# Expert gathers in a two-layer PEER model: down and up rows side by side, one 8 KB gather per pick in eight slots, two picks at a time

## The chip, the cores and the metric

One core of a Trainium2 chip runs the whole program. The metric is device time in microseconds (us). Each run of the kernel before gives one time; three runs were made.

## The reference

The model has two layers and a third part with sparse attention, linear attention and a mixture of experts. The change touches only the feed-forward of the two layers, which looks up single rows of large tables:

```
def peer_ffn(h, w_q, sub_keys, down, up):
    def one_block(xb):                          # 128 tokens; there are two such blocks
        q = (xb @ w_q).reshape(n, 8, 2, 128)    # 8 heads, 2 halves of a key
        s = einsum('thpk,pnk->thpn', q, sub_keys)
        s_top, i_top = top_k(s, 16)
        ... the best 16 of the 16 x 16 sums -> idx, gate = softmax(best_s)
        u = take(down, idx, axis=0)             # 16 picks for each of 8 heads, rows of 1024 floats
        act = gelu(einsum('thkd,td->thk', u, xb))
        v = take(up, idx, axis=0)
        return einsum('thk,thkd->td', gate * act, v)
```

Each token picks 8 heads x 16 = 128 experts out of 16384. For each of them it needs a row of `down` (4 KB in float32), whose dot product with the token gives a weight, and the row of `up` with the same index (4 KB), which is added to the output with that weight. A layer has 256 tokens, so 128 picks x 2 blocks of 128 tokens = 256 gathers of `down` and 256 of `up`, each of 128 rows (512 KB): 268 MB in a layer.

## The kernel before

The program is written engine by engine, with semaphores between them. In each layer `peer(l)` does this part. Tokens lie on the 128 partitions; `t` is the block of 128 tokens, a group `g` (0 to 15) is one head of one block, and `k` (0 to 15) is a pick within it. So a gather brings, for one (g, k), one row to each partition.

**GpSimd (POOL)** issues all gathers as indirect DMAs in the order of `gather_order()`: first the 16 down rows of group 0, then down rows of group g and up rows of group g-1 in turn, and the 16 up rows of the last group at the end. There are 16 slots of 4 KB a partition (`gslot`): eight in `G_arena`, eight in two buffers of the weight ring that are lent to the gathers for the length of the stage. Before the gather number i is issued, POOL waits until the gather i-16 has been used: by DVE if it was a down row, by TensorE if it was an up row. Slots 8 to 11 are open from query 1 on, slots 12 to 15 from query 3 on, since the ring buffers hold the query weights until then.

**DVE** does the dots (`down(g)`, one `scalar_tensor_tensor` of 128x1024 with an accumulated sum, line 1253). Between the dots it works off the search for the next heads' indices, `top_k`, in 15 steps, one after each of the first three picks of every four. At the end of a group it does `weight(g)`: the 16 activations times the gates. At the end of the layer `mix_last` adds eight of the last 16 up rows on DVE.

**ScalarE (ACT)** applies gelu to the 16 dots of a group at once, and then makes the diagonals (line 823): for each pick a 128x128 matrix with that pick's weights on its diagonal, in four buffers.

**TensorE (PE)** multiplies the diagonal by the up row, two matmuls of 512 columns for each pick (line 1971), and sums all 128 picks of a block in two PSUM banks. A float32 matmul shows as two records. Ahead of this, PE runs the eight queries (`query(s)`, line 1714, 64 records each) and their scores (line 1927), all before the first up row.

**Layer 0 has more in it**: in the shadow of the gathers PE works out the modulation of layer 1 (`mod_parts`, line 1771, and `mod_total`), one of 10 chunks at the end of each group from group 4 on. ACT copies their results out (lines 702 and 709), and SP loads the weights of a later chunk (2 MB, line 548) when the semaphore `modp` says that a chunk is used. Layer 1 has two such chunks.

At the end `add_experts` multiplies the two banks of a block by a gain and adds them to `x`.

Of the kernel before, what the change touches and what calls it, by code (L numbers as in the profile page):

```python
# [22 lines left out]
NT = T // P  # L23
# [8 lines left out]
GSLOTS = 16  # L32
# [43 lines left out]
def query_no(l, s):  # L76

    return 9 * l + s + 2
# [28 lines left out]

def hidden(l, g):

    c = HIDDEN[l].start + g - SHADOW  # L110
    return [c] if c in HIDDEN[l] else []


def gather_order():

    order = [("down", 0, k) for k in range(GSLOTS)]
    for g in range(1, BLOCKS):
        for k in range(GSLOTS):
            order += [("down", g, k), ("up", g - 1, k)]
    return order + [("up", BLOCKS - 1, k) for k in range(GSLOTS)]  # L120


ORDER = gather_order()
PLACE = {pick: i for i, pick in enumerate(ORDER)}


LAST_MIXED = (1, 3, 5, 7, 9, 11, 12, 13)
LAST_UP = tuple(k for k in range(GSLOTS) if k not in LAST_MIXED)
UPS = GSLOTS * (BLOCKS - 1) + len(LAST_UP)


def up_picks(g):

    return range(GSLOTS) if g < BLOCKS - 1 else LAST_UP


def up_no(l, g, k):

    return UPS * l + GSLOTS * g + up_picks(g).index(k) + 1

# [65 lines left out]
def program(nc, a, out):  # L206

    ctx = ExitStack()
    with ctx:
# [93 lines left out]
        G_arena = pe_(8, D)  # L303
# [7 lines left out]
        mixed_up = qb.rearrange("p a b c -> p (a b c)")[:, D:2 * D]  # L311
# [49 lines left out]
        def lend(l):  # L361

            lent[l] = turn[0:2]
            for _ in range(2):
                enter(None, ("x_peer", NT * (l + 1)))
            for k in lent[l]:
                turn.remove(k)
# [47 lines left out]
        def gslot(l, kind, g, k):  # L415

            n = PLACE[kind, g, k] % GSLOTS
            if n < 8:
                return G_arena[:, n]
            return ring[:, lent[l][(n - 8) // 4], 1024 * (n % 4):1024 * (n % 4) + 1024]  # L420

        def wait_gathered(eng, l, kind, g, k):
            i = PLACE[kind, g, k]
            eng.wait_ge(S[f"gathered{i % GSLOTS}"], 16 * ((len(ORDER) * l + i) // GSLOTS + 1))

# [99 lines left out]
        def _(sp):  # L525
# [62 lines left out]
            sp.wait_ge(S["up_used"], UPS)  # L588
# [10 lines left out]
            sp.wait_ge(S["up_used"], 2 * UPS)  # L599
# [30 lines left out]
        @block.gpsimd  # L630
        def _(pool):
            for l in range(2):
                for i, (kind, g, k) in enumerate(ORDER):
                    t, hh = g // 8, g % 8
                    if kind == "down" and k == 0:
                        pool.wait_ge(S["idx_ready"], 9 * l + (g // 2 + 2 if g else 1))
                    if i >= GSLOTS:
                        before, of, j = ORDER[i - GSLOTS]
                        if before == "down":
                            pool.wait_ge(S["down_used"], GSLOTS * (BLOCKS * l + of) + j + 1)  # L640
                        else:
                            pool.wait_ge(S["up_used"], up_no(l, of, j))
                    elif i >= 8 and i % 4 == 0:
                        pool.wait_ge(S["pq"], query_no(l, 2 * ((i - 8) // 4) + 1))
                    elif l and i == 0:
                        pool.wait_ge(S["x_peer"], NT * l)
                    pool.indirect_dma_start(  # L647
                        out=gslot(l, kind, g, k), out_offset=None, in_=a[kind],
                        in_offset=bass.IndirectOffsetOnAxis(ap=idx_all[:, t, 16 * hh + k:16 * hh + k + 1], axis=0)).then_inc(
                        S[f"gathered{i % GSLOTS}"], 16)  # L650
# [3 lines left out]
        def _(act_):  # L654
# [110 lines left out]
            def peer(l):  # L765
# [39 lines left out]
                for s in range(2, 8):  # L805
                    query_out(s)
                    score_out(s - 1)
                score_out(7)

                def gelu(g):  # L810
                    t, hh = g // 8, g % 8
                    part = act[:, t, 16 * hh:16 * hh + 16]
                    act_.wait_ge(S["down_used"], GSLOTS * (BLOCKS * l + g + 1))
                    act_.activation(part, part, ACT.Gelu_apprx_tanh).then_inc(S["peer_gelu"], 1)

                def diagonals(g):
                    t, hh = g // 8, g % 8
                    act_.wait_ge(S["peer_w"], BLOCKS * l + g + 1)
                    for k in up_picks(g):
                        n = up_no(l, g, k)  # L820
                        if n > 4:
                            act_.wait_ge(S["up_used"], n - 4)
# [3 lines left out]
                for g in range(BLOCKS + 1):  # L826
                    if g < BLOCKS and g % 2 == 0:
                        t, c = g // 8, (g // 2) % 4
                        part = gate[:, t, 32 * c:32 * c + 32]
                        act_.wait_ge(S["gate_in"], 8 * l + g // 2 + 1)  # L830
                        act_.activation(part, part, ACT.Exp).then_inc(S["gate_exp"], 1)
                    if g:
                        diagonals(g - 1)
                    if g < BLOCKS:
                        gelu(g)
                    if l == 0 and g == 11:
                        act_.wait_ge(S["x_peer"], 1)
                        tile_sum(x, h, 0)
                    if l == 0 and g == 13:
                        tile_root("n1_1", 0)  # L840
                    if g == BLOCKS:
                        root_table()
                    for c in hidden(l, g - 1):
                        mod_part_out(1, c, 0)
                    for c in hidden(l, g - 2):
                        mod_total_out(1, c, 0)
# [132 lines left out]
        def _(v):  # L979
# [205 lines left out]
            def peer(l):  # L1185
# [54 lines left out]
                def gates(m):  # L1240
# [5 lines left out]
                    link(v.tensor_tensor(g3, g3, bc(gsum[:, 1], 2, 16), ALU.mult))  # L1246

                def down(g):
                    t, hh = g // 8, g % 8
                    for k in range(GSLOTS):  # L1250
                        row = gslot(l, "down", g, k)
                        wait_gathered(v, l, "down", g, k)
                        v.scalar_tensor_tensor(out=row, in0=row, scalar=1.0, in1=h[:, t], op0=ALU.mult,  # L1253
                                               op1=ALU.mult, accum_out=act[:, t, 16 * hh + k:16 * hh + k + 1]).then_inc(
                            S["down_used"], 1)
                        n = GSLOTS * (g % 2) + k
                        if g < BLOCKS - 2 and n % 4 < 3 and n - n // 4 < STEPS:
                            top_k(g // 2 + 1, n - n // 4)

                def weight(g):  # L1260
                    t, hh = g // 8, g % 8
                    v.wait_ge(S["peer_gelu"], BLOCKS * l + g + 1)
                    part = act[:, t, 16 * hh:16 * hh + 16]
                    v.tensor_tensor(part, part, gate[:, t, 16 * hh:16 * hh + 16], ALU.mult).then_inc(S["peer_w"], 1)

                def add_experts(t):
                    v.wait_ge(S["up_used"], up_no(l, 7, GSLOTS - 1) if t == 0 else UPS * (l + 1))
# [4 lines left out]

                def mix_last():
                    t, g = NT - 1, BLOCKS - 1
                    v.wait_ge(S["peer_w"], BLOCKS * (l + 1))
                    for i, k in enumerate(LAST_MIXED):
                        w = act[:, t, 16 * (g % 8) + k:16 * (g % 8) + k + 1]
                        wait_gathered(v, l, "up", g, k)
                        if i:
                            link(v.scalar_tensor_tensor(out=mixed_up, in0=gslot(l, "up", g, k), scalar=w, in1=mixed_up,  # L1280
                                                        op0=ALU.mult, op1=ALU.add))
                        else:
                            link(v.tensor_scalar(mixed_up, gslot(l, "up", g, k), w, None, ALU.mult))
                    link(v.tensor_tensor(mixed_up, mixed_up, mod[:, 5], ALU.mult))
                    link(v.tensor_tensor(x[:, t], x[:, t], mixed_up, ALU.add))
# [5 lines left out]
                for g in range(BLOCKS):  # L1291
                    down(g)
                    if g % 2 == 0:
                        gates(g // 2)
                    weight(g)
# [7 lines left out]
                    if l == 0 and g == 14:  # L1303
# [5 lines left out]
                        tile_norm("n1_1", 0, x, h, mod[:, 1], mod[:, 0])  # L1309
                if l == 0:  # L1310
# [6 lines left out]
                v.wait_ge(S["pq_ev"], query_no(l, 7))  # L1317
# [1030 lines left out]
```

## Time and profile before

| | |
|---|---|
| three runs | 2755.77, 2758.12 and 2764.55 us, median 2758.12 us |
| profiled execution | span 2868.3 us from its first to its last instruction |
| instructions | 22121 |
| gather stage of layer 0 | first gather issued at 282.0 us, last up row's matmuls end at about 1083 us |
| gather stage of layer 1 | first gather at 1131.7 us, last up row's matmuls end at 1919.9 us |
| busy shares of the span | PE 79%, DVE 41%, ACT 17%, POOL 39% |
| queue of the gathers | 536.94 MB, 49.3% of what 16 DMA engines could do in the span |

The profiled execution is 110 us longer than the median of the three runs. All rows are from it. The line numbers are those of the kernel before. A DMA share of 1.0 means that all 16 DMA engines had packets all the time; GB/s is what they moved. "PEclk" is the granted TensorE clock as a share of full speed: 1.00 is 2.4 GHz and 0.50 is 1.2 GHz. "Idle before" is the time in which an engine did nothing ahead of an instruction, and the arrow names what ended it; "issue" means nothing that the profile shows, "remote" another core or a queue that it does not know.

### The profile page before, as it was taken

Reading aid. Unit: us, or ns where it says so; the run is one execution under the profiler, and the core shown is the slowest. Engines: PE = TensorE matmul, PEld = TensorE weight load, DVE = VectorE, ACT = ScalarE, POOL = GpSimd, SP = SyncE. Lnnn points to the kernel's source line nnn. Section 1 sums busy time; section 2 is a strip of 40 time slices with the busy share of each in tenths; the row PEclk is TensorE's granted clock in tenths of the full one; section 3 lists DMA queues with packets and bytes.
Section 4 is the critical chain, followed back from the end, with each engine's and each line's share of the span. In section 5 each row is a group of like instructions: output and inputs, shape, how many; then the busy total and the mean of one; then the engine's idle time right before and its main releaser. Section 6 shows DMA issues by size and latency. Waiting matters only on the chain.

```text
span 2868.3 us, 22121 instructions
## 1 busy us (share of the span) xinstructions
PE 2268.7 (79%) x7843; PEld 1064.3 (37%) x7843; DVE 1180.9 (41%) x2875; ACT 494.1 (17%) x1074; POOL 1117.8 (39%) x1028
## 2 busy tenths in 40 slices
PE   6998876676776877977567776759997989998997
PEld 2455722222232336722123222224454544344443
DVE  1243665555556445665556555440043421010101
ACT  2141111121111211211111111120124111000001
POOL 0000577776776761577767777750000000000000
PEclk9998899988898888999979998989998889999999
DMA  8433899999999985899979999994410059999996
GB/s 321 164 140 119 287 365 368 353 401 385 383 401 396 378 335 199 288 355 360 382 288 356 364 374 351 377 340 155 171 66 0 1 221 393 393 395 393 393 393 245
DMA packets 292278, 864.12 MB, mean 301 GB/s; under 512 B 19372, under 2 KB 26668, under 8 KB 291912
## 3 DMA queue, kind: packets, MB, share of 16 engines
q0 software_dynamic: 147456, 536.94, 49.3%
q1 hardware_dynamic: 144712, 325.74, 30.5%
q8 instruction: 66, 1.08, 0.2%
q14 instruction: 44, 0.36, 0.0%
HBM read 861.55 MB, written 1.05 MB: 301 GB/s over the span
## 4 chain that ended last, share of the span: by engine, by line
PE 43%; DMA 16%; POOL 16%; issue 11%; another core or an unknown queue 5%; DVE 4%; ACT 3%; SPq 2%; POOLq 0%; DVEq 0%; ACTq 0%
PE bank L1714 17%; PE bank L1971 12%; DMA arena<-in_w_up 9%; POOL ring L647 8%; POOL arena L647 8%; DMA ring<-in_up,arena 5%; PE bank L2223 5%; PE bank L1723 2%; SPq L619 2%; DMA arena<-in_up,arena 2%; PE bank L1771 1%; PE bank L2266 1%; PE bank L1783 1%; PE bank L1784 1%
## 5 line engine op out<-in xcount | busy, mean ns | idle before, releaser
L1971 PE MATMUL bank<-arena 128*128 128x512 f32 x992 | 508.2, 654 | 228.8 <-ACT arena L823 112.5
L1971 PE MATMUL bank<-ring,arena 128*128 128x512 f32 x992 | 496.7, 635 | 170.7 <-DMA ring<-in_up,arena 100.4
L1253 DVE SCALAR_TENSOR_TENSOR ring<-ring,h 128x1024 f32<-128x1024 f32 x256 | 313.0, 1225 | 307.8 <-DMA ring<-in_down,arena 233.4
L647 POOL DMA_INDIRECT arena<-in_down,arena x256 | 261.6, 1022 | 439.4 <-DVE arena L1237 348.7
L1253 DVE SCALAR_TENSOR_TENSOR arena<-arena,h 128x1024 f32<-128x1024 f32 x256 | 313.5, 1226 | 263.4 <-DMA arena<-in_down,arena 179.5
L1971 PEld LDWEIGHTS bank<-arena 128*128 128x128 f32 x992 | 193.8, 207 | 540.5 <-issue 380.7
L1971 PEld LDWEIGHTS bank<-ring,arena 128*128 128x128 f32 x992 | 182.1, 197 | 478.1 <-issue 269.0
L647 POOL DMA_INDIRECT arena<-in_up,arena x256 | 288.2, 1126 | 146.5 <-PE bank L1971 61.5
L823 ACT ACTIVATE arena<-const,arena 128x128 f32<-128x128 f32 x496 | 188.3, 398 | 855.0 <-PE bank L1971 500.2
L647 POOL DMA_INDIRECT ring<-in_up,arena x256 | 292.7, 1143 | 103.8 <-issue 68.6
L647 POOL DMA_INDIRECT ring<-in_down,arena x256 | 275.1, 1074 | 104.3 <-issue 77.4
L1714 PE MATMUL bank<-ring,hT 128*128 128x512 f32 (+2 forms) x640 | 256.0, 563 | 3.0 <-ACT hT L693 2.2
L2223 PE MATMUL bank<-ring,arena 128*64 128x512 f32 x768 | 233.3, 604 | 29.2 <-DMA arena<-in_w_up 28.0
L1714 PEld LDWEIGHTS bank<-ring,hT 128*128 128x128 f32 x640 | 124.4, 195 | 133.1 <-issue 125.3
L1678 DVE TENSOR_TENSOR arena<-arena,bank 128x512 f32<-128x512 f32 x16 | 11.0, 689 | 341.1 <-PE bank L2223 341.1
L1714 PE MATMUL bank<-hT,ring 128*128 128x128 f32 x1024 | 130.5, 289 | 15.9 <-issue 12.8
L2223 PEld LDWEIGHTS bank<-ring,arena 128*64 128x64 f32 x768 | 73.0, 139 | 178.7 <-issue 177.3
L1714 PEld LDWEIGHTS bank<-hT,ring 128*128 128x128 f32 x1024 | 127.2, 205 | 18.7 <-issue 16.5
L2223 PE MATMUL bank<-arena 128*64 128x512 f32 x256 | 121.3, 630 | 0.0
L2266 PE MATMUL bank<-ring,arena 128*64 128x512 f32 x256 | 113.3, 595 | 9.1 <-DVE arena L1680 9.1
L2266 PE MATMUL bank<-arena 128*64 128x512 f32 x256 | 113.3, 595 | 0.0
L1723 PE MATMUL bank<-const 128*128 128x512 f32 x186 | 88.1, 630 | 0.0
(400 smaller groups left out, 1873.5 us busy)
## 6 DMA issues: line engine op xcount, KB each, us to landing
ring<-in_w_gate SPq DMA_DIRECT2D x32, 2048.0 KB, 22.3
ring<-in_mod_w SPq DMA_DIRECT2D x24, 2048.0 KB, 15.2
ring<-in_w_up SPq DMA_DIRECT2D x16, 2048.0 KB
arena<-in_w_up SPq DMA_DIRECT2D x16, 2048.0 KB, 19.9
ring<-in_w_down SPq DMA_DIRECT2D x16, 2048.0 KB, 14.3
arena<-in_w_down SPq DMA_DIRECT2D x16, 2048.0 KB, 19.0
ring<-in_w_in SPq DMA_DIRECT2D x9, 2048.0 KB, 7.6
ring<-in_peer_w_q SPq DMA_DIRECT2D x8, 2048.0 KB, 11.5
```

The source lines that it names most:

```text
L619: sp.dma_start(w_moe[3 * k + j].rearrange("p (k n) -> p k n", k=kk), a[w][2 * i + k].rearrange("(k p) n -> p k n", p=P)).then_inc(moe_land ...
L647: pool.indirect_dma_start(out=gslot(l, kind, g, k), out_offset=None, in_=a[kind], in_offset=bass.IndirectOffsetOnAxis(ap=idx_all[:, t, 16 ...
L823: act_.activation(diag[:, n % 4], ident, ACT.Copy, scale=act[:, t, 16 * hh + k:16 * hh + k + 1]).then_inc(S["diag_made"], 1)
L1253: v.scalar_tensor_tensor(out=row, in0=row, scalar=1.0, in1=h[:, t], op0=ALU.mult, op1=ALU.mult, accum_out=act[:, t, 16 * hh + k:16 * hh + ...
L1714: ins = pe.matmul(dst, lhsT, rhs, start=i == 0, stop=i == len(pairs) - 1)
L1723: pe.matmul(bank[b][:, :], ones, cst("causal"), start=True, stop=True)
L1771: ins = pe.matmul(bank[4 * l + n % 2][32 * j:32 * j + 32, :], (cB2 if ctx else cB)[:, 2 * j + k], w[:, 2 * j + k], start=k == 0, stop=k == ...
L1783: pe.matmul(bank[4 * l + 2 + n % 2][:, :], ones, mpart[:, n % 2], start=True, stop=False)
L1784: pe.matmul(bank[4 * l + 2 + n % 2][:, :], ones[row:row + 1], bias, start=False, stop=True).then_inc(S["mod"], 1)
L1971: ins = pe.matmul(bank[2 * t + c][:, :], diag[:, n % 4], row[:, 512 * c:512 * c + 512], start=hh == 0 and k == 0, stop=hh == 7 and k == up ...
L2223: ins = pe.matmul(bank[2 + j][CAP * k:CAP * k + CAP, :], xs[:, q, CAP * k:CAP * k + CAP], w_k[3 * k + j][:, q], start=q == 0, stop=q == KT ...
L2266: ins = pe.matmul(bank[c][CAP * k:CAP * k + CAP, :], hsel[:, f, CAP * k:CAP * k + CAP], w_k[3 * k + 2][:, f, 512 * c:512 * c + 512], start ...
```

## The change

- The host lays `down` and `up` side by side in one table, `experts`, of 8 KB rows. One gather per pick brings both rows (1 MB in all). A layer issues 256 gathers and not 512.
- There are eight slots of 8 KB in the place of 16 of 4 KB. The bytes are the same.
- The work goes in groups `j` of two picks (`PER = 2`), 128 to a layer. POOL waits before every second gather, and for TensorE alone: the pair of slots is free when the up matmuls of the pair four places earlier are done (`slot_free`).
- ACT applies gelu to two dots at a time (`weigh`) and makes no diagonals.
- DVE makes the diagonals, with activation and gate multiplied in the same `tensor_scalar`, right behind the dots of the next pair: `diagonals(j-1)` follows the second dot of pair `j`. It waits for the gelu of its pair and, since there are two pairs of diagonal buffers, for the matmuls of two pairs earlier.
- PE does the matmuls of a pair on one wait. Queries 4 to 7 move from ahead of the stage to behind pairs 3, 7, 11 and 15, and their scores one pair later.
- `mix_last` goes: all up rows are summed on PE.
- SP's loads that waited for query 7 and for the last up row wait for the same events, at their new places.

```diff
-GSLOTS = 16
+GSLOTS = 8
+HEAD = 16
...
+LATE_QUERIES = {3: 4, 7: 5, 11: 6, 15: 7}
...
+PER = 2
+GROUPS = PICKS * NT // PER
+
+def slot_free(l, n):
+    return GROUPS * l + (n - GSLOTS) // PER + 1
...
-        G_arena = pe_(8, D)
+        G_arena = pe_(4, 2 * D)
...
                 # GpSimd
+                for n in range(PICKS * NT):
...
+                    if n >= GSLOTS:
+                        if n % PER == 0:
+                            pool.wait_ge(S["up_used"], slot_free(l, n))
+                    elif n >= 4 and n % 2 == 0:
+                        pool.wait_ge(S["pq"], query_no(l, n - 3))
...
                     pool.indirect_dma_start(
-                        out=gslot(l, kind, g, k), out_offset=None, in_=a[kind],
+                        out=gslot(l, n), out_offset=None, in_=a["experts"],
...
                 # ScalarE
+                def weigh(j):
+                    t, at = PER * j // PICKS, PER * j % PICKS
+                    part = act[:, t, at:at + PER]
+                    act_.wait_ge(S["down_used"], GROUPS * l + j + 1)
+                    act_.activation(part, part, ACT.Gelu_apprx_tanh).then_inc(S["peer_gelu"], 1)
...
-                        act_.activation(diag[:, n % 4], ident, ACT.Copy, scale=act[:, t, 16 * hh + k:16 * hh + k + 1]).then_inc(
-                            S["diag_made"], 1)
...
                 # DVE
+                def diagonals(j):
+                    t, at = PER * j // PICKS, PER * j % PICKS
+                    v.wait_ge(S["peer_gelu"], GROUPS * l + j + 1)
+                    if j % HEAD == 0:
+                        v.wait_ge(S["gates"], 8 * l + j // HEAD + 1)
+                    if j >= 2:
+                        v.wait_ge(S["up_used"], GROUPS * l + j - 1)
+                    for k in range(PER):
+                        ins = v.tensor_scalar(diag[:, PER * (j % 2) + k], ident, act[:, t, at + k:at + k + 1],
+                                              gate[:, t, at + k:at + k + 1], ALU.mult, ALU.mult)
+                    ins.then_inc(S["diag_made"], 1)
...
                 def down(g):
+                    for k in range(HEAD):
+                        row = gslot(l, HEAD * g + k)[:, 0:D]
+                        wait_gathered(v, l, HEAD * g + k)
...
+                        if k % PER == PER - 1:
+                            ins.then_inc(S["down_used"], 1)
+                            if g or k >= PER:
+                                diagonals((HEAD * g + k) // PER - 1)
...
-                def weight(g):
-                def mix_last():
...
                 # TensorE
+                for j in range(GROUPS):
...
+                    pe.wait_ge(S["diag_made"], GROUPS * l + j + 1)
+                    for k in range(PER):
+                        row = gslot(l, PER * j + k)[:, D:2 * D]
...
+                    ins.then_inc(S["up_used"], 1)
+                    if j in LATE_QUERIES:
+                        query(LATE_QUERIES[j])
+                    if j - 1 in LATE_QUERIES:
+                        scores(LATE_QUERIES[j - 1])
```

## Rows read from the trace of the kernel before

**Rows 1.** The page: span, POOL and PE busy, the gathers' queue.
```profile
span 2868.3 us, 22121 instructions
PE 2268.7 (79%) x7843; PEld 1064.3 (37%) x7843; DVE 1180.9 (41%) x2875; ACT 494.1 (17%) x1074; POOL 1117.8 (39%) x1028
...
q0 software_dynamic: 147456, 536.94, 49.3%
```

**Rows 2.** Busy time by stretch: engine busy us (count), last PEclk, DMA share, GB/s.
```profile
282.00:350.00 68.00, 57.25 (x464) 55.50 (x463) 41.11 (x132) 12.55 (x22) 38.85 (x33) 0.91 0.76 266
350.00:600.00 250.00, 179.91 (x371) 64.97 (x369) 148.35 (x358) 42.05 (x102) 190.08 (x170) 0.96 0.98 367
600.00:1050.00 450.00, 336.97 (x790) 127.85 (x788) 246.22 (x552) 82.48 (x193) 316.56 (x302) 0.89 1.00 390
1200.00:1900.00 700.00, 498.34 (x1005) 183.49 (x1004) 391.37 (x905) 116.23 (x281) 516.27 (x471) 0.92 0.95 357
```

**Rows 3.** Timeline of layer 1, a steady stretch: start, length, engine, instruction, idle before.
```profile
1401.46 1.48 POOL L647 DMA_INDIRECT ring<-in_down,arena  x1 [0.30 <-issue]
...
1402.19 1.98 PE L1971 MATMUL bank<-arena 128*128 128x512 f32 x4 [0.57 <-DMA arena<-in_up,arena]
...
1407.04 0.99 POOL L647 DMA_INDIRECT ring<-in_down,arena  x1 [0.30 <-issue]
...
1408.34 0.94 POOL L647 DMA_INDIRECT ring<-in_up,arena  x1 [0.31 <-issue]
1408.56 1.23 DVE L1253 SCALAR_TENSOR_TENSOR ring<-ring,h 128x1024 f32<-128x1024 f32 x1 [1.33 <-DMA ring<-in_down,arena]
...
1409.58 1.02 POOL L647 DMA_INDIRECT ring<-in_down,arena  x1 [0.30 <-issue]
```

**Rows 4.** Groups of instructions between 1200 and 1900 us: busy, mean ns, idle before.
```profile
L1229 DVE TENSOR_TENSOR cols<-const,cols 128x512 f32<-128x512 f32 x14 | 9.6, 689 | 0.0
...
L1041 DVE MATCH_REPLACE8 gvec<-cols,gvec 128x128 f32<-128x128 f32 x16 | 4.3, 276 | 1.3 <-issue 1.3
...
L1217 DVE TENSOR_SCALAR cols<-cols 128x32 uint32<-128x32 uint32 x6 | 1.0, 174 | 0.0
```

**Rows 5.** Timeline of layer 1 around a restart of the gathers.
```profile
1490.53 0.60 ACT L702 ACTIVATE hT<-bank 128x512 f32<-128x512 f32 x1 [19.88 <-remote]
...
1492.05 10.09 PE L1971 MATMUL bank<-arena 128*128 128x512 f32 x16 [15.72 <-ACT arena L823]
...
1495.84 0.40 ACT L823 ACTIVATE arena<-const,arena 128x128 f32<-128x128 f32 x1 [3.07 <-PE bank L1971]
1496.08 0.94 POOL L647 DMA_INDIRECT arena<-in_up,arena  x1 [7.20 <-PE bank L1971]
1497.32 0.94 POOL L647 DMA_INDIRECT arena<-in_down,arena  x1 [0.30 <-issue]
...
1502.57 1.23 DVE L1253 SCALAR_TENSOR_TENSOR arena<-arena,h 128x1024 f32<-128x1024 f32 x1 [7.11 <-DMA arena<-in_down,arena]
```

**Rows 6.** Two stretches of 2 us in the mixture of experts: 2 KB rows, then 4 KB rows.
```profile
2396.00:2398.00 2.00, 1.43 (x10) 0.63 (x10) 1.80 (x6) 0.85 (x2) 0.00 (x0) 1.00 1.03 383
2414.00:2416.00 2.00, 2.00 (x10) 0.77 (x11) 0.00 (x0) 0.00 (x0) 0.00 (x0) 1.00 1.03 412
```

**Rows 7.** Timeline of PE in layer 0: queries 4 and 5 and their neighbours' scores.
```profile
310.68 7.31 PE L1714 MATMUL bank<-hT,ring 128*128 128x128 f32 x64
317.82 1.06 PE L1927 MATMUL bank<-cols,arena 128*128 128x128 f32 x8
318.72 7.31 PE L1714 MATMUL bank<-hT,ring 128*128 128x128 f32 x64
325.86 1.06 PE L1927 MATMUL bank<-cols,arena 128*128 128x128 f32 x8
```

**Rows 8.** Stretches of 10 us: eight of layer 1's 70 are under 300 GB/s.
```profile
1260.00:1270.00 10.00, 9.93 (x17) 4.28 (x18) 9.86 (x23) 2.06 (x6) 8.18 (x7) 0.70 0.76 252
...
1490.00:1500.00 10.00, 7.95 (x12) 3.46 (x13) 2.47 (x4) 3.04 (x8) 2.81 (x3) 0.60 0.50 177
...
1880.00:1890.00 10.00, 8.82 (x15) 3.37 (x14) 3.91 (x9) 2.41 (x6) 6.42 (x7) 0.64 0.86 297
```

**Rows 9.** Waits of ACT, layer 0, then layer 1: us in total, times, longest.
```profile
ACT hT L702 <- remote: 92.3, 8, 18.7
...
ACT hT L702 <- remote: 40.4, 2, 20.5
```

**Rows 10.** Timeline of the end of layer 1's gathers.
```profile
1911.03 0.94 POOL L647 DMA_INDIRECT ring<-in_up,arena  x1 [0.30 <-issue]
...
1916.21 3.70 PE L1971 MATMUL bank<-ring,arena 128*128 128x512 f32 x8 [3.13 <-DMA ring<-in_up,arena]
...
1921.45 1.22 DVE L1271 TENSOR_TENSOR x<-x,arena 128x1024 f32<-128x1024 f32 x1
```

More of the change, by code:

```diff
@@ L111, in hidden @@
     return [c] if c in HIDDEN[l] else []
[L114 to L139, printed above, removed]
+PER = 2
+GROUPS = PICKS * NT // PER
+def slot_free(l, n):
+    return GROUPS * l + (n - GSLOTS) // PER + 1
 def operand(tag, n):
@@ L587, in _ @@
             load_gain(4)
-            sp.wait_ge(S["up_used"], UPS)
+            sp.wait_ge(S["up_used"], GROUPS)
             load_weights("pool", 1)
@@ L826, in peer @@
[L826 to L836, printed above, removed]
+                query_out(2)
@@ new lines, in peer, with gate_out @@
+                score_out(1)
+                query_out(3)
+                score_out(2)
+                score_out(3)
+                def weigh(j):
+                    t, at = PER * j // PICKS, PER * j % PICKS
+                    part = act[:, t, at:at + PER]
+                    act_.wait_ge(S["down_used"], GROUPS * l + j + 1)
+                    act_.activation(part, part, ACT.Gelu_apprx_tanh).then_inc(S["peer_gelu"], 1)
+                def gate_out(m):
+                    t, c = m // 4, m % 4
+                    part = gate[:, t, 32 * c:32 * c + 32]
+                    act_.wait_ge(S["gate_in"], 8 * l + m + 1)
+                    act_.activation(part, part, ACT.Exp).then_inc(S["gate_exp"], 1)
@@ new lines, in peer @@
+                gate_out(0)
+                for j in range(GROUPS):
+                    g, i = j // 8, j % 8
+                    weigh(j)
+                    if j in LATE_QUERIES:
+                        query_out(LATE_QUERIES[j])
+                    if j - 1 in LATE_QUERIES:
+                        score_out(LATE_QUERIES[j - 1])
+                    if j % HEAD == 8 and j // HEAD < 7:
+                        gate_out(j // HEAD + 1)
+                    for c in hidden(l, g - 1):
+                        if i == 1:
+                            mod_part_out(1, c, 0)
+                        if i == 5:
+                            mod_total_out(1, c, 0)
+                    if l == 0 and (g, i) == (11, 0):
@@ L837, in peer @@
                         act_.wait_ge(S["x_peer"], 1)
                         tile_sum(x, h, 0)
-                    if l == 0 and g == 13:
+                    if l == 0 and (g, i) == (13, 0):
                         tile_root("n1_1", 0)
[L841 to L846, printed above, removed]
+                root_table()
@@ L1248, in down @@
                 def down(g):
                     t, hh = g // 8, g % 8
[L1250 to L1258, printed above, removed]
@@ L1260, in weight @@
-                def weight(g):
[L1261 to L1264, printed above, removed]
+                    for k in range(HEAD):
+                        row = gslot(l, HEAD * g + k)[:, 0:D]
+                        wait_gathered(v, l, HEAD * g + k)
+                        ins = v.scalar_tensor_tensor(out=row, in0=row, scalar=1.0, in1=h[:, t], op0=ALU.mult,
+                                                     op1=ALU.mult, accum_out=act[:, t, HEAD * hh + k:HEAD * hh + k + 1])
+                        if k % PER == PER - 1:
+                            ins.then_inc(S["down_used"], 1)
+                            if g or k >= PER:
+                                diagonals((HEAD * g + k) // PER - 1)
+                        n = HEAD * (g % 2) + k
+                        if g < BLOCKS - 2:
+                            if n % 4 < 3 and n - n // 4 < STEPS:
+                                top_k(g // 2 + 1, n - n // 4)
+                            if n == 24:
+                                gates(g // 2 + 1)
+                        if g == 0 and k == 1:
+                            gates(0)
@@ L1309, in peer @@
                         tile_norm("n1_1", 0, x, h, mod[:, 1], mod[:, 0])
+                diagonals(GROUPS - 1)
                 if l == 0:
```

129 lines of the change are left out of this document (45 added, 84 removed).

## The prediction

> **What bounds the kernel now.** I read the page first. PE is the busiest engine by the share of the span, and the gathers' queue holds 49.3% of the DMA engines' time [rows 1]. Busy time by stretch puts that share where it belongs: in both gather stages the DMA engines stand at 0.95 to 1.00 while PE is at about 0.7, so these stages, 55% of the span, are paced by the gathers [rows 2]. The timeline of a steady stretch shows two limits that fall together. POOL issues a gather every 1.24 to 1.31 us and waits for nobody between (idle 0.30 us each time): two gathers in 2.54 us. That is 1.05 MB in 2.54 us, 413 GB/s, and 410 GB/s is also about what the DMA engines reach elsewhere with 4 KB rows [rows 3, 6]. A down row issued at 1401.46 us is used at 1408.56 us, 7.1 us later. Its slot is needed again only 16 gathers (20 us) after its issue. So before, a slot has some 12 us to spare.
>
> Layer 1 between 1200 and 1900 us moves 357 GB/s, not 410 [rows 2]: 13% or 90 us are lost. Eight stretches of 10 us under 300 GB/s hold 35 us of it [rows 8]; they are restarts after a wait like that of ACT on line 702 [rows 5]. The other 55 us are POOL's: 471 issues took 516 us, 1.10 us each against 0.94 undisturbed [rows 2, 3], and with 0.30 between them that is 1.40 us a gather where the DMA engines need 1.28.
>
> **What goes.** 256 of 512 POOL issues in a layer. POOL then needs 1.4 us for a pick of which the transfer takes 2.56, so it paces nothing any more. At most this returns the 55 us in layer 1, and less in layer 0, where the 2 MB weight loads from another queue fill the DMA engines (390 GB/s). ACT's diagonals, `weight` and `mix_last` go too. They lie beside the transfers and are worth nothing in the sum.
>
> **What it costs: the loop.** A slot is now held from its issue until PE has used the pair, and diagonals of pair j wait for the dots of j+1. So the gathers of pair j+4 are issued after the matmuls of j, and those need pair j+1 landed: one turn of the loop moves the work on by three pairs. Its terms, with an otherwise quiet queue:
> - PE's end to POOL's issue: 0.25 us (1495.84, when ACT is let go, to 1496.08) [rows 5].
> - Issue to use of a gather of 0.5 MB: 5.25 us (1497.32 to 1502.57), and 5.2 us for the last one (1911.03 to 1916.21) [rows 5, 10]. For 1 MB I add 1.28 us, and 2.56 us for the second of the pair behind the first: 9.05 us. The bound above is the 7.1 us of the full queue in place of 5.2 [rows 3], 11 us; the bound below is 8 us, if a microsecond of the 5.2 was the gather ahead.
> - The second dot: 1.23 us [rows 3].
> - Two diagonals on DVE. No row shows a `tensor_scalar` of 128x128 in float32. It lies between 0.17 us (128x32) and 0.28 us (another operation of 128x128) [rows 4]. I take 0.22, 0.45 us a pair; the ends are 0.35 and 0.55.
> - The way to PE 0.1 us, and two picks of 1.98 us that overlap by 0.26: 3.7 us [rows 3].
>
> Sum: 14.8 us for three pairs, 4.9 a pair. On top comes what DVE has in hand when the second row lands. A step of `top_k` is 0.9 to 2.1 us (three operations of 0.69 us in the longest) [rows 4] and goes behind 15 of 32 picks. The row may have to wait for it, or POOL's first issue may take 1.5 us. I put 0.8 us on a turn: 15.6 us, 5.2 us a pair. The DMA engines need 2.10 MB / 410 GB/s = 5.1 us for a pair. Two limits so close do not simply give the larger one; any late step on either side is kept. I take 5.25 us (bounds 5.0 and 5.9).
>
> The diagonal is also the place where the Trainium skill speaks against the change: "SBUF — State Buffer", in its list of which operations grab the shared port pair, says that a float32 `tensor_scalar` within SBUF can keep GpSimd from writing descriptors. POOL's issues do range up to 1.48 us beside DVE's work [rows 3]. By the rule an issue that met both diagonals would take 0.45 us more, and by the loop's order none meets its own pair's, since POOL is waiting for PE then; the sum would be the same by both.
>
> **What it costs: the start.** Before, 18 MB have moved 68 us after the first gather (266 GB/s) [rows 2]. After, the last two of eight slots open when query 3 ends, at 310.7 us [rows 7], and are full at 317; no slot comes free before PE's first pair. DVE can weigh that pair once the scores and the exponentials of the gates are out, some 5 us behind query 3. Four pairs at about 4.1 us of DVE (two dots, two diagonals, one or two steps) and 5.5 us from dot to matmuls put pair 3's end at 337, 55 us after the first gather. Then four queries stand in the loop, each 7.15 us, and four scores of 0.9 to 1.06 [rows 7]. From pair 3 the matmuls of pair 4 wait for query 4 (R + 10.9 us), then 9.3 us for the gather of pair 8 and 5.5 for the dots, diagonals and matmuls of pair 7: 25.7 us for four pairs, and not 21. Four such rounds end with pair 19 at 55 + 103 = 158 us. The remaining 108 pairs at 5.25 us are 567 us: 725 us a layer. In layer 0 ten weight loads of 2 MB add 5.1 each, 52 us. The end is even: last landing to `x` takes 1.23 + 0.45 + 3.8 + 2.7 = 8.2 us, before 6.5 [rows 10].
>
> **The sum.** In the profile, layer 1's stage is 788 us before. After it is 725 us, plus the gaps. These hold 35 us today and stay, since what makes them (the waits on line 702 and their like) is not touched, and each restart now begins with a whole pair at half clock, as PE's first 16 records take 10.1 us where four at full clock take 1.98 [rows 5, 3], with no slot in hand: 3 us more each. So 725 + 35 + 24 = 784, no change. Layer 0 comes to 725 + 52 + 25 = 802 against 801. But the profiled execution is 110 us above the median run. It is likeliest that this excess lies in the waits without a visible cause: line 702 alone waits 92 us in layer 0 and 40 in layer 1 [rows 9]. Then before, a timed run spends about 1589 - 110 = 1479 us in both stages, and after, with no gaps, 2 x 725 + 52 = 1502: 23 us slower. If the excess lies elsewhere, the change is worth nothing. I take 22 us: 2758 + 22 = 2780 us.
>
> **The rivals.**
> - *The loop is longer.* If a gather of a pair lands like one of the full queue (11 us and not 9.05), a turn is 17.5 us, 5.85 a pair: 216 x 0.6 = 130 us more, 2890. Half of that is 2840. For it: the loop has no slack, and a weight load in layer 0 doubles the time of a transfer. Against: the queue is shallower, with at most 4 MB waiting of 8. It decides from a turn of 16.5 us up.
> - *Faster: the loop stays under the transfers.* If the landing takes 8 us and DVE's steps hide in the 2.5 us between two rows, a turn is 14.3 us and the DMA engines pace. Going from 2 KB to 4 KB rows took them from 383 to 412 GB/s [rows 6], which is 10 us of fixed time per 1000 packets; with 8 KB it would be 424, 4.95 us a pair. 216 x 0.3 = 65 us less than my sum, 2715. It decides below a turn of 15 us. "DMA: Bandwidth & Descriptors" of the Trainium skill (Anatomy of one DMA) would have it so: 2.0 us fixed plus bytes at 436 GB/s, by which an estimate for the second of the pair is 6.8 us. The rows have 5.2 us for half a megabyte, where that rule gives 3.2.
> - *Faster: the gaps shrink.* Line 702's waits grow while POOL goes on filling 16 slots (8 MB, 20 us of transfers). Now POOL stops after a pair or two. If the waits are also in the timed runs, and half of their 132 us goes with half of the depth, that is up to 50 us: 2710 to 2745. Against: the chain behind them has no slack, so what is shorter in the wait is paid in the restart.
> - *No change*: gains on POOL and losses at the start cancel, as in the profile's sum: 2750 to 2766.
>
> **Numbers.** Slower as forecast (2767 to 2830) 0.35, longer loop 0.17, no change 0.13, transfers pace 0.20, gaps shrink 0.15. What a measurement can tell from no change is 0.3%, 8 us. Faster 0.35, same 0.13, slower 0.52. The range leaves out 0.1 on either side: 2695 to 2870. The likeliest case alone is 2767 to 2830.
>
> **What would show it.** Right: POOL's gathers in steady stretches wait for PE (line 1971 renamed), not 0.30 "issue"; DMA share between 0.93 and 0.99 there; first issue of a pair to its second dot about 9 us; pairs every 5.2 us; in the first 16 pairs PE is nearly always busy and POOL idle for 7 us around each query. Wrong: a DMA share of 1.0 at over 415 GB/s with POOL's waits short of the transfers (faster), or landings of 11 us with shares under 0.9 (much slower). What would break the forecast most is the landing term, since each microsecond in it is a third of a microsecond a pair, 72 us in all, and the part of the 110 us excess that timed runs have too.

## The result

The changed kernel takes 2874.22 us (median of four runs, 2868.83 to 2882.88); the kernel before took 2761.34 us beside it (2755.77 to 2765.86). The ratio is 1.042, 95% interval [1.039, 1.045]: 113 us slower, where 22 were forecast, and 4 us above the end of the range. A later set of seven runs gave 2873.83 us again, but the kernel before stood at 2853.16 us in that set, ratio 1.007 [1.005, 1.009]. So the kernel before has two levels, near 2758 and near 2853 us, one to each set of runs (a set ran on one chip); the changed kernel showed one in these two sets.

First the page of the changed kernel, answering to [rows 1].

```profile
span 2867.0 us, 21606 instructions
PE 2301.3 (80%) x7907; PEld 1094.2 (38%) x7907; DVE 1283.7 (45%) x3335; ACT 350.3 (12%) x802; POOL 565.1 (20%) x516
...
q0 software_dynamic: 73728, 536.90, 47.5%
```

POOL's work is halved and half the packets carry the same bytes, yet the span of this execution is that of the profiled one before (2868.3 us). Busy time by stretch, answering to [rows 2]; the columns are engine busy us (count), PEclk, DMA share, GB/s.

```profile
282.00:440.00 158.00, 126.52 (x621) 83.51 (x620) 89.13 (x263) 16.80 (x40) 44.55 (x44) 0.92 0.77 293
440.00:600.00 160.00, 117.28 (x239) 45.62 (x238) 105.07 (x263) 12.17 (x35) 58.92 (x54) 0.90 0.96 381
600.00:1050.00 450.00, 340.97 (x793) 131.27 (x792) 290.39 (x727) 38.81 (x110) 179.72 (x151) 0.92 0.98 386
1134.00:1300.00 166.00, 132.42 (x648) 88.17 (x646) 94.43 (x280) 16.80 (x40) 45.05 (x46) 0.93 0.74 288
1300.00:1900.00 600.00, 436.93 (x880) 171.20 (x881) 398.23 (x998) 40.62 (x128) 226.86 (x209) 0.91 0.95 373
```

Long after the start, layer 1 moves 373 GB/s, a pair (2.10 MB) in 5.62 us. The forecast had 5.25. No engine is full. The waits of that last stretch say who waits for whom (us in total, times, longest; those of ACT and of PE's weight loads are left out):

```profile
POOL ring L631 <- PE bank L1948: 180.1, 52, 8.6
PE bank L1948 <- DVE arena L1237: 164.7, 81, 4.7
POOL arena L631 <- PE bank L1948: 155.1, 52, 8.0
DVE ring L1246 <- DMA ring<-in_experts,arena: 117.5, 97, 4.1
DVE arena L1246 <- DMA arena<-in_experts,arena: 82.8, 79, 3.9
```

That is a closed ring: POOL waits for PE, PE for DVE's diagonals, DVE for the transfers, and these for POOL. The timeline of layer 1, a stretch without steps of `top_k` (start, length, engine, instruction, idle before), answers to [rows 3]:

```profile
1846.26 1.86 POOL L631 DMA_INDIRECT ring<-in_experts,arena  x1 [2.50 <-PE bank L1948]
1847.23 0.60 DVE L1237 TENSOR_SCALAR arena<-const,arena 128x128 f32<-128x128 f32 x2
...
1847.88 3.70 PE L1948 MATMUL bank<-ring,arena 128*128 128x512 f32 x8 [1.90 <-DVE arena L1237]
1848.42 0.94 POOL L631 DMA_INDIRECT ring<-in_experts,arena  x1 [0.30 <-issue]
...
1851.86 1.56 POOL L631 DMA_INDIRECT ring<-in_experts,arena  x1 [2.49 <-PE bank L1948]
...
1855.14 1.23 DVE L1246 SCALAR_TENSOR_TENSOR ring<-ring,h 128x1024 f32<-128x1024 f32 x1 [2.01 <-DMA ring<-in_experts,arena]
...
1857.63 1.23 DVE L1246 SCALAR_TENSOR_TENSOR ring<-ring,h 128x1024 f32<-128x1024 f32 x1 [1.26 <-DMA ring<-in_experts,arena]
...
1858.78 0.60 DVE L1237 TENSOR_SCALAR arena<-const,arena 128x128 f32<-128x128 f32 x2
...
1859.44 3.70 PE L1948 MATMUL bank<-arena 128*128 128x512 f32 x8 [2.55 <-DVE arena L1237]
```

Follow one turn. The pair issued at 1846.26 has its dots at 1855.14 and 1857.63, 8.9 and 11.4 us later, both ended by the transfers. Then come the diagonals of the pair ahead of it, 3.70 us of PE, and at 1863.41 the next issue into slots of this turn: 17.15 us, three pairs further on, 5.7 us each.

### The profile page after: what moved, and what is told of

Read it like the earlier page. It is cut to its first block, busy times and chain, and to the rows that moved or that the text cites. A ratio compares the mean times of both kernels' runs of the same rounds, so it can differ in the third digit from the quotient of the medians.

```text
span 2867.0 us, 21606 instructions
## 1 busy us (share of the span) xinstructions
PE 2301.3 (80%) x7907; PEld 1094.2 (38%) x7907; DVE 1283.7 (45%) x3335; ACT 350.3 (12%) x802; POOL 565.1 (20%) x516
## 4 chain that ended last, share of the span: by engine, by line
PE 46%; DMA 33%; DVE 7%; issue 6%; POOL 3%; ACT 3%; SPq 2%; DVEq 0%; POOLq 0%; ACTq 0%
PE bank L1948 16%; PE bank L1691 16%; DMA arena<-in_experts,arena 13%; DMA ring<-in_experts,arena 10%; DMA arena<-in_w_up 10%; PE bank L2206 5%; PE bank L1700 2%; SPq L602 2%; DVE arena L1237 2%; POOL ring L631 1%; PE bank L1748 1%; POOL arena L631 1%; DVE arena L1246 1%; PE bank L1760 1%; PE bank L1761 1%
## 5 line engine op out<-in xcount | busy, mean ns | idle before, releaser
L1948 PE MATMUL bank<-ring,arena 128*128 128x512 f32 x1024 | 535.5, 674 | 219.2 <-DVE arena L1237 219.2
L631 POOL DMA_INDIRECT arena<-in_experts,arena x256 | 275.9, 1078 | 858.5 <-PE bank L1948 469.3
L1948 PEld LDWEIGHTS bank<-ring,arena 128*128 128x128 f32 x1024 | 210.6, 214 | 540.9 <-DVE arena L1237 308.2
L631 POOL DMA_INDIRECT ring<-in_experts,arena x256 | 289.0, 1129 | 478.9 <-PE bank L1948 416.8
L1948 PEld LDWEIGHTS bank<-arena 128*128 128x128 f32 x1024 | 200.2, 205 | 473.4 <-DVE arena L1237 258.9
L799 ACT ACTIVATE arena<-arena 128x2 f32<-128x2 f32 x256 | 51.1, 203 | 1205.6 <-DVE ring L1246 621.3
L1237 DVE TENSOR_SCALAR arena<-const,arena 128x128 f32<-128x128 f32 x512 | 153.6, 343 | 79.8 <-ACT arena L799 79.3
L1691 PE MATMUL bank<-hT,ring 128*128 128x128 f32 x1024 | 123.9, 284 | 3.0 <-ACT hT L759 3.0
L1748 PE MATMUL bank<-ring,hT 128*32 128x512 f32 x448 | 60.6, 669 | 13.6 <-DMA ring<-in_mod_w 12.8
## 6 DMA issues: line engine op xcount, KB each, us to landing
ring<-in_mod_w SPq DMA_DIRECT2D x24, 2048.0 KB, 17.2
```

The source lines that it names most:

```text
L631: pool.indirect_dma_start(out=gslot(l, n), out_offset=None, in_=a["experts"], in_offset=bass.IndirectOffsetOnAxis(ap=idx_all[:, t, at:at + ...
L1237: ins = v.tensor_scalar(diag[:, PER * (j % 2) + k], ident, act[:, t, at + k:at + k + 1], gate[:, t, at + k:at + k + 1], ALU.mult, ALU.mult)
L1691: ins = pe.matmul(dst, lhsT, rhs, start=i == 0, stop=i == len(pairs) - 1)
L1748: ins = pe.matmul(bank[4 * l + n % 2][32 * j:32 * j + 32, :], (cB2 if ctx else cB)[:, 2 * j + k], w[:, 2 * j + k], start=k == 0, stop=k == ...
L1948: ins = pe.matmul(bank[2 * t + c][:, :], diag[:, PER * (j % 2) + k], row[:, 512 * c:512 * c + 512], start=j % (GROUPS // NT) == 0 and k == ...
```

## The experiments

Each is the changed kernel with one edit, except where it says so.

**The kernel before, twice more.** Nothing edited.

> The kernel before, unchanged, for one more profile. If the 107 to 110 us by which its first profiled execution stood above its timed runs belong to its form under the profiler (ACT's waits on line 702, 92 us in one layer and 40 in the other), they come back: span near 2868 us, the same waits within 20 us each. If they were an accident of one execution, the span is near 2760 and those waits are gone or small.

It took 2753.03 us, and the profile's span was 2751.2 us. The second one:

> The kernel before once more, to see which of its two levels it is at here: near 2755 us without waits put down to a remote releaser, or near 2860 with some 130 us of them on line 702.

This took 2852.41 us. Line 702, the waits of `before_again`, then of `e11_before_third`:

```profile
  PE bank L1771: 83.1, 25
```

```profile
  remote: 113.9, 9
  PE bank L1771: 55.1, 16
```

"Remote" does not mean another core here. Line 702 waits for `modp`, which PE raises with its last matmul of line 1771. In the profile that the prediction read, PE's records of that line end at 1474.2 us, and ACT begins only at 1490.53 us [rows 5], 16.3 us later; in `before_again` it begins 0.07 us after them, in each of the 12 cases in the gather stages.

```profile
1472.30 1.92 PE L1771 MATMUL bank<-ring,hT 128*32 128x512 f32 x16
```

```profile
1393.23 1.92 PE L1771 MATMUL bank<-ring,hT 128*32 128x512 f32 x16
...
1395.22 0.60 ACT L702 ACTIVATE hT<-bank 128x512 f32<-128x512 f32 x1 [3.65 <-PE bank L1771]
```

So at the upper level ACT stands still while PE, by its records, is done. The ends of matmuls are modelled in the profile, so it does not tell whether PE finished late or its signal came late.

Stretches at the two levels, `before_again` first:

```profile
600.00:1050.00 450.00, 362.12 (x853) 133.21 (x852) 255.76 (x539) 89.31 (x210) 313.28 (x298) 0.95 1.01 399
1300.00:1800.00 500.00, 379.54 (x785) 132.56 (x786) 300.86 (x671) 91.44 (x218) 381.40 (x370) 0.98 1.01 393
```

```profile
600.00:1050.00 450.00, 338.52 (x790) 128.00 (x788) 244.49 (x548) 83.91 (x195) 317.70 (x299) 0.89 0.99 384
1300.00:1700.00 400.00, 284.76 (x588) 103.00 (x587) 232.33 (x562) 67.05 (x161) 301.96 (x276) 0.94 0.96 360
```

So the excess of 110 us in the profile that the prediction read was a level of the kernel before, with these waits as its mark, and the timed runs beside it did not have it. At the lower level the two gather stages take 753 us (first gather at 284.5, end of the last up row's matmuls at 1038.0) and 717 us (1086.4 to 1803.2).

**Own dots.** Each pair's diagonals come right behind its own dots, so no pair waits for the next pair's gathers.

```
-                            if g or k >= PER:
-                                diagonals((HEAD * g + k) // PER - 1)
+                            if g == 0 and k == PER - 1:
+                                gates(0)
+                            diagonals((HEAD * g + k) // PER)
...
-                diagonals(GROUPS - 1)
```

> The changed kernel with each pair's diagonals made right behind that pair's own dots, so no pair waits for the next pair's gathers. Theory (the loop over slots sets the pace): the turn stays near 17.1 us but now moves the work on by four pairs, 4.3 us a pair, below what the transfers need (5.1), so the pace becomes about 5.1 to 5.2 in place of 5.65 and the time falls by 216 x 0.5 = 100 us or more, to 2740 to 2790 us. Rival (8 KB rows, the late queries or DVE's added work are slow by themselves, whatever the order): the pace stays within 0.1 us of 5.65 and the time within 25 us of 2874. Second rival (DVE now waits for ACT's Gelu behind each pair, some 0.8 us, and dots come late): 2850 or slower.

2733.10 us (eight runs), ratio to before at its lower level 0.991 [0.987, 0.994], 7 us below my range. 141 us of the 2874 are gone with one edit of order, at the same rows, slots, queries and operations on DVE. Pairs 20 to 127 of layer 1 take 5.10 us each; the queue is now full, and a landing takes 14.1 us in the mean. Layer 0 of it, and for comparison the same stretch above at 381:

```profile
440.00:600.00 160.00, 120.83 (x276) 46.70 (x276) 118.79 (x303) 13.14 (x39) 72.35 (x61) 0.97 1.01 419
```

That puts both rivals out: 8 KB rows move at 419 GB/s when enough of them are under way. A repeat of the same kernel (there is no second diagonal in it, whatever its label says):

> A second look at the kernel with each pair's diagonals behind its own dots: 2733 us within 8 us, and 415 GB/s in the steady stretch.

It took 2737.98 us, in a set where the kernel before stood at its upper level. So this variant does not have that level either.

**Groups of one pick.**

```
-PER = 2
+PER = 1
-LATE_QUERIES = {3: 4, 7: 5, 11: 6, 15: 7}
+LATE_QUERIES = {7: 4, 15: 5, 23: 6, 31: 7}
...
-                    if j >= 2:
-                        v.wait_ge(S["up_used"], GROUPS * l + j - 1)
+                    if j >= 4:
+                        v.wait_ge(S["up_used"], GROUPS * l + j - 3)
```

> The changed kernel with groups of one pick instead of two (the lag is then one pick and a slot is freed by each pick). Theory of the loop: a turn of about 0.3 + 9 to 10 (one landing) + 1.2 + 0.5 + 0.1 + 1.9 = 13 to 14 us moves the work on by seven picks, 3.8 to 4.0 us a pair, below the 5.1 of the transfers: the transfers pace, 2740 to 2790 us. Rival (8 KB rows are slow by themselves): within 25 us of 2874. Rival (twice the handshakes between DVE, ACT and PE cost more than the finer slots give): 2860 or slower.

2725.95 us, 0.988 [0.982, 0.994]: the fastest kernel of the study, and 14 us below my range. The lag is one pick now, and a slot comes free with each pick. Layer 1, where the changed kernel has 0.91, 0.95 and 373:

```profile
1300.00:1800.00 500.00, 385.91 (x819) 136.29 (x818) 357.24 (x881) 62.09 (x220) 195.03 (x179) 0.98 0.98 403
```

(The stage ends inside that stretch; the stretches of 25 us between 1325 and 1750 hold 406 to 424 GB/s.)

**Queries ahead of the loop**, as before.

```
-LATE_QUERIES = {3: 4, 7: 5, 11: 6, 15: 7}
+LATE_QUERIES = {}
-                query(2)
-                scores(1)
-                query(3)
-                scores(2)
-                scores(3)
+                for s in range(2, 8):
+                    query(s)
+                    scores(s - 1)
+                scores(7)
```

> The changed kernel with all eight queries ahead of the loop, as before. The first 16 pairs lose the wait for queries of 7 us each in both layers (the step of the prediction that puts pair 19 at 158 us), but the first pairs start some 30 us later. Theory: the sum of the two is small, -30 to +20 us, and the steady pace of 5.65 us a pair stays. Rival (the late queries carry most of the loss): 80 us or more faster.

2877.58 us, 3 us from the changed kernel. Pair 3 ends 81 us after the first gather and not 51, pair 19 at 165 and 172 us and not 167 and 168. What the late queries give the first pairs they take from the next sixteen.

**Diagonals written twice.**

```
+                    for k in range(PER):
+                        link(v.tensor_scalar(diag[:, PER * (j % 2) + k], ident, act[:, t, at + k:at + k + 1],
+                                             gate[:, t, at + k:at + k + 1], ALU.mult, ALU.mult))
```

> The changed kernel with two more operations on DVE per pair: each pair's diagonals are written twice, the first two one after the other with a wait between. That is some 0.7 to 0.8 us more on the way from a pair's dots to its matmuls (0.60 us now). Theory (the loop sets the pace, one turn moves on three pairs): a third of that a pair, 0.23 to 0.27 us, 215 pairs: 50 to 60 us slower than 2874, so 2925 to 2935; if longer gaps also take PE's clock down more often, up to 2960. Rival (DVE or the transfers set the pace by their rate): DVE is 60% busy in the stage and the transfers do not change, so within 10 us of 2874.

2957.69 us, 84 us more, above the 50 to 60 and inside the larger bound. Over pairs 16 to 123 of layer 1 the mean from the second dot's start to the diagonals grows from 1.17 to 2.00 us, and from there to the next issue from 5.18 to 5.39; the landing is 10.7 us against 10.8. That is 0.92 us a turn, 0.31 a pair. In layer 0 the same terms give 0.66 us a turn, 0.22 a pair. Together that is some 57 us for the 108 later pairs of both layers, and the first 32 gathers of each layer take 20 us more together: 77, where the two profiled executions are 79 us apart. So what DVE takes on the way is paid nearly in full (0.83 us added, 0.92 and 0.66 measured), a third to each pair, though DVE is idle a third of the stage.

**A matmul behind each pair, to hold the clock.** In 20-us stretches of the changed kernel's layer 1 from 1310 us on, the gathers move 390 GB/s where the granted clock is 0.95 or more, 369 between 0.85 and 0.95, and 352 below. (With the stretches laid 10 us earlier it is 386, 366 and 365, so the last step is an accident of where they begin.) After a gap, PE's pair can take 5.4 us in place of 3.7, as in this row of the timeline:

```profile
1894.98 5.40 PE L1948 MATMUL bank<-ring,arena 128*128 128x512 f32 x8 [4.47 <-DVE arena L1237]
```

I took this for a cause.

```
+                    if 2 <= g < 8 or 11 <= g < 15:
+                        keep_warm(1, 2 - 2 * t)
```

> The changed kernel with one matmul of 128x512 on constants put behind each pair's matmuls in blocks 2 to 7 and 11 to 14 (80 of 128 pairs of a layer), into a bank that is not in use; the computation is not changed. PE is then busy some 0.9 us more per pair and its gaps are shorter. Theory A (half-clock pairs are a large part of what was missed: in 20-us stretches of layer 1 the gathers move 391 GB/s where the granted clock is 0.95 or more, 370 at 0.85 to 0.95 and 352 below): the clock rises to 0.97 or more in those blocks, the pace there from 5.64 to about 5.36 us a pair, 160 x 0.28 = 45 us faster, 2830. Theory B (the clock falls because of the late transfers and costs little itself): within 10 us of 2874, or slower by up to 20 us where a pair waits for the added matmul.

2864.61 us, 10 us less than the changed kernel's two medians: theory A, which had 2830, is wrong. The clock did as I wanted (the changed kernel has 0.92 and 0.90 in these two stretches) and the rate hardly moved (386 and 371 GB/s there):

```profile
600.00:1050.00 450.00, 369.69 (x900) 145.91 (x901) 290.09 (x725) 39.45 (x109) 173.14 (x151) 0.97 0.98 388
1300.00:1700.00 400.00, 317.10 (x699) 126.12 (x698) 277.98 (x714) 30.61 (x89) 161.17 (x140) 0.97 0.96 372
```

The way from diagonals to next issue fell by 0.16 us (layer 1), and the landing rose by as much, 10.84 to 11.00. So the low clock comes with the gaps that late transfers leave on PE, and taking it away gave some 10 us, net of the added matmul's own time.

**Half of PE's work.** One half of the up rows' products is left out.

```
-                        for c in range(2):
+                        for c in (k,):
```

> The changed kernel with half of PE's work in the loop: of each pair the first pick is added to the first 512 columns alone and the second pick to the last 512 alone; the other half of the up rows' products is left out. A pair on PE takes 1.85 us in place of 3.70. Theory (PE's time is part of the loop): 1.85 / 3 = 0.62 us less per pair, until the transfers pace at 5.1 to 5.2: 2755 to 2790 us, near the variant with own dots; somewhat more if the lower load on PE takes the granted clock down. Rival (PE's time lies beside the loop, and only the transfers' latency counts): within 20 us of 2874.

2792.96 us, 81 us less and 3 us above my range: PE's time is part of the ring. PE ran at 0.73 of full clock, so only 1.16 us of the 1.85 went from each turn, and 0.56 of that came back as a longer landing (11.4 us, layer 1).

```profile
1300.00:1700.00 400.00, 234.11 (x337) 73.02 (x337) 289.67 (x762) 28.65 (x90) 171.21 (x148) 0.73 0.98 387
```

**Own dots, diagonals twice.** The edits of both kernels.

> The variant with own dots, and each pair's diagonals written twice (0.7 to 0.8 us more between a pair's dots and its matmuls, on DVE). Theory: four pairs a turn leave the loop below the transfers (turn some 17.5 us, the transfers need 20.2 for four pairs), so the added 0.8 us is hidden: 2733 to 2745 us. Rival (DVE's time counts wherever it is added, as it did without own dots): 50 us or more slower, 2785 or more.

2787.11 us, 50 us more than own dots alone, so my expectation failed; the time is the one that the rival gave. In one stretch of 20 us of layer 1, this kernel and then own dots:

```profile
1460.00:1480.00 20.00, 15.75 (x33) 6.03 (x31) 18.37 (x41) 3.62 (x7) 7.21 (x6) 0.91 0.91 353
```

```profile
1460.00:1480.00 20.00, 15.45 (x31) 6.04 (x30) 16.83 (x53) 0.81 (x4) 9.28 (x8) 0.91 1.01 422
```

DVE is busy 18.4 of 20 us; what is left is the 0.27 us before each pair's diagonals, its wait for ACT. In most stretches up to 1740 us it stands between 17 and 19, and it has next to no waits for transfers (18 us in 400). Own dots without it has DVE at 13 to 18. In layer 1 the later pairs slow down from 5.10 to 5.26 us, 18 us in all, and for these DVE's rate where steps of `top_k` run is the likely bound, a reason that neither theory had named. It does not explain the rest: of the 56 us between the two profiled executions, 19 and 18 arise before pair 19 ends, where the late queries stand in the loop and DVE is busy 63% of the time, and layer 0's later pairs lose nothing (5.51 us, 5.50 before). There the rival's reason may hold; no run separates it.

**Own dots and one pick together**, both edits.

> Both edits together: groups of one pick, and each pick's diagonal right behind its own dot. If the transfers already set the pace in each of the two (415 to 419 GB/s in steady stretches), the sum brings nothing in the steady stretch: 2715 to 2730 us. If DVE's wait for Gelu behind every pick (0.6 us) costs dots, 2735 or more.

2742.70 us, beside 2737.98 for own dots in the same set: no gain from the second edit, as the transfers pace both (419 GB/s between 1300 and 1700 us), and 5 us lost. Against one pick alone 17 us are lost. The loss lies in the first 20 pairs: pair 19 ends 160 us after the first gather, with own dots 153, with one pick 149; the later pairs are no slower (5.06 us in layer 1, 5.10 in the two others). That these are ACT and DVE meeting 256 times a layer and not 128 is argued, not shown.

**The changed kernel again.**

> The changed kernel, unchanged, for its spread. The kernel before took 2758 us in one set of runs and 2853 in another, while the variant with own dots took 2733 and 2738. If the changed kernel is as little touched by that as the variants, it takes 2874 us within 10, and its ratio to before depends on which level before is at: 1.04 against 2758, 1.007 against 2853. If it has two levels too, some 2970 shows up.

2873.83 us; no second level.

## Why the prediction was wrong

**The mechanism was right.** A loop of three pairs, closed by POOL waiting for PE, sets the pace; own dots, one pick, diagonals twice and half of PE each moved the time the way that the loop has it. What came is the rival "the loop is longer", which I gave 0.17; its condition (a landing of 11 us, a turn over 16.5) is met. Its price was added up wrongly: 2780 + 130 is 2910 and not 2890, and half of it 2845. The 2874 measured lie between.

**The step that failed is the landing term.** I took 9.05 us "with an otherwise quiet queue" and set 0.8 beside it for DVE: 9.85. From the starts of all 256 issues and dots of a layer, the mean over pairs 16 to 123 is 10.84 us in layer 1 and 11.55 in layer 0. The 9.05 is right for a quiet queue, by the one case looked at: in layer 0's first restart the two gathers are used 5.4 and 9.2 us after the first issue:

```profile
316.40 0.94 POOL L631 DMA_INDIRECT arena<-in_experts,arena  x1 [13.24 <-PE bank L1948]
...
321.82 1.23 DVE L1246 SCALAR_TENSOR_TENSOR arena<-arena,h 128x1024 f32<-128x1024 f32 x1 [3.19 <-DMA arena<-in_experts,arena]
```

(The second dot started at 325.57.) But the queue is quiet only there: at a pace of 5.25 us a pair and 5.1 us of transfer, the pair issued before is still moving. I had said that two limits so close do not give the larger one, and then put 0.05 us on it. Half of PE and the matmul behind each pair show the same from the other side: the landing grows when the rest of the turn shrinks. How this wait divides between the queue and the engines finishing out of step was not measured.

**The rest of the turn.** It adds 0.6 us, less than the landing's 1.0 (layer 1) and 1.7 (layer 0). Two diagonals are 0.60 us and not 0.45 (343 ns each, above my 0.22 and my upper end). PE is 3.7 us in most pairs, as taken; with half-clock pairs the mean from diagonals to next issue is 5.18 against 4.5. Dot to diagonals 1.17 (without pair 16, whose diagonals wait 7 us), forecast 1.23. The sum is 17.2 us in layer 1 and 17.9 in layer 0, forecast 15.6.

**Where the 94 us are** (2874 - 2780). Layer 1's stage is 781 us against 725: pair 19 ends at 168 us, forecast 158, +10; 108 pairs at 5.68, forecast 5.25, +46. Layer 0's is 807 against 777: pair 19 +9, the rest +21, its weight loads costing 27 us more than layer 1 and not 52. That is 86 of the 94. Of the other 8, 5 come from the profiled execution being that much below the median (2868.83 us against 2874.22), and 3 lie outside the two stages.

**The profile's sum.** I had 784 and 802 us for the stages, "no change" in the profile, and 781 and 807 came. That agreement is two errors against each other: the 59 us of gaps and restarts that I carried over into layer 1 are hardly there (line 702's successor waits 3.7 us in layer 1), and the pace ate them. The argument that the 110 us lay in waits which a timed run lacks was right for before: 753 + 717 = 1470 us, forecast 1479. For after it meant that the profile's 784 and 802 could not both contain gaps and equal a timed run; "no gaps, 1502" was the right form, against 1588 measured, with a pace 0.4 us too short in layer 1.

**Points that held.** With 8 KB rows the transfers can go faster: own dots moves 415 to 419 GB/s in steady stretches (424 were worked out for 8 KB rows), before 393 to 399 at its lower level. How much of that POOL's halved work gives and how much the longer rows, no run separates. Pair 3 at 51 us, forecast 55. The late queries even out. The gaps-shrink rival has its waits gone, but against the timed runs there was nothing to shrink.

**The port.** The prediction said, beside the Trainium skill's "SBUF — State Buffer" (which operations grab the shared port pair), that no issue meets its own pair's diagonals. They meet the pair ahead's, as in the timeline above. Between 1300 and 1700 us, POOL's issues beside no work of DVE take 0.94 us (all 19), those beside dots alone 1.00, those that overlap the diagonals 1.23 (45 of 138, longest 1.94); between 480 and 1050 us of layer 0, 1.35 (68). The rule agrees in direction with these: 0.3 to 0.4 us each, in 27 of the 45 on the first issue of a pair, and so inside the landing. An estimate by the Trainium skill's "DMA: Bandwidth & Descriptors" (Anatomy of one DMA) has the second gather land in 6.8 us; the runs have 9.2 us in a quiet queue and 10.8 in the steady loop.

**Left open.** Why ACT gets PE's signal late at the upper level of the kernel before. The lower level came on chip 5, the upper one on chips 0 and 7, so it may belong to the chip, but the chips of the first runs and of the profile are not on record. The kernels of 8 KB rows were free of it on all three. With it stays open what the change costs in general: 113 us against one level, 21 against the other.

## What to carry to other kernels

Before pricing a loop over slots, count how many groups a turn moves on: a lag of one group took one of four and cost 141 us, where the change without the lag gains 25 us. Where the loop's turn comes near what the transfers need (here 15.6 us forecast against 15.3), price a landing as that of a busy queue, and take the term from the steady stretch, not from a restart. Ask for a second profile where the profiled execution stands 4% above the timed runs, before arguing about where that excess lies.

## What the runs showed of the hardware

One indirect gather of 128 rows of 8 KB reached its use in 5.4 us when the queue was quiet. 8 KB rows move at 415 to 419 GB/s with the queue kept full, and at 373 to 386 with a DMA share of 0.95 to 0.98 when it is refilled two gathers at a time. A `tensor_scalar` of 128x128 float32 with two scalars from memory takes 343 ns, more than the 0.28 us of the neighbour that I had as upper bound. PE's granted clock followed the loop (0.91 in the changed kernel, 0.98 with one pick, 0.73 with half of its work); raising it from 0.90 to 0.97 in a stretch of the loop left the rate at 371 to 372 GB/s.
